# Last projection of a decoder step with the tokens stationary and the rows of b_w_out streaming

## Chip, cores and metric

The kernel runs on one core of a Trainium2 chip. The metric is the device time of the whole program in microseconds (us), as the median of several runs. The engines are PE (TensorE: PE its matmuls, PEld its weight loads), ACT (ScalarE), DVE (VectorE), POOL (GpSimd) and SP (SyncE, which here only issues DMAs). Every engine works through its own instructions in order and waits on semaphores for the others.

## What is computed

One inference step of a two-layer decoder: 512 prompt tokens and 8 sample tokens, model width 1024, float32. Layer 0 is a state-space mixer, layer 1 a dilated attention with a gate. The change touches the end of layer 1 alone:

```python
    o = o.reshape(bsz, seq_len, ATTN_WIDTH).astype(x.dtype) * jax.nn.silu(z)
    return x + rms_norm(o @ w_out, norm_post)
...
def rms_norm(x, g):
    xf = x.astype(jnp.float32)
    y = xf * lax.rsqrt(jnp.mean(xf * xf, axis=-1, keepdims=True) + RMS_EPS)
    return (y * g.astype(jnp.float32)).astype(x.dtype)
```

Here `o` is 520 tokens by 1024, `w_out` (the input b_w_out) 1024 by 1024, and the mean runs over the 1024 outputs of a token. The results y_prompt and y_sample are token rows of 1024.

## The kernel before, in words

**Number format.** Every large product is made of three: operands are split into a high part (fp32r, a copy by ACT) and a low part (the difference to the original, a subtraction by POOL for weights and by DVE for activations), and PE adds high x high, high x low and low x high in PSUM.

**Layout.** Activations lie with channels on the 128 partitions and the 520 tokens along the row. The residual stream is `xT`, 8 tiles of 128 channels x 520 tokens. PSUM holds two accumulators of 1024 columns (`acc`) and four of 512 (`aux`).

**A projection before** (class `Dense`, lines 76 to 194). Weights come in units of 128 x 1024 (8 blocks of 128 inputs x 128 outputs) into two slots `raw`; ACT makes `w_hi` (L104), POOL `w_lo` (L109), and PE multiplies with the weight block stationary and the tokens moving in two cuts of 256 and 264 columns (L161, in the mixer L1950). One unit gives one output tile of 128 channels: 8 blocks x 3 terms x 2 cuts = 48 matmuls. Units alternate between the two slots and the two accumulators.

**The mixer** (function `mixer`, L1539 on) holds the kv projection, the q projection with the attention of the prompt, the gate projection (tiles Z0 to Z0+7) and, spread among them, the attention of the 8 sample tokens. Its order is written out by hand, tile by tile and slot by slot, for each engine. At its end:
- SP issues the v rows of the sample attention (`v_rows`), and before the last four of them it waits for POOL's last splits, to load the first two units of b_w_out (L1782).
- PE runs `value_rows(0)` between the last two gate tiles and `value_rows(1)` after the last (L1900, L1903: 32 columns of probabilities stationary, 512 columns moving), then `pick_heads` (L1913: 128 x 128 stationary, 8 columns moving, 16 products that the trace shows as 32 matmuls).
- DVE makes `ot` = attention x gate (`gate`, L2050) and the low part `ylo` (`low`, L2054), ACT the high part `yhi` (`high`, L2239). The sample's columns come last: `pick_heads`, a copy (L2154), the gate (L2158), the high part (L2289), the low part (L2160).

**After the mixer** come two functions with blocks of their own, and between blocks the engines meet:
- `attn_out` calls `residual` (L1379): 8 units of b_w_out as above. DVE copies each output tile out of PSUM (L1497), ACT squares it (L284), and PE sums the squares over the channels by a product with a matrix of ones (L290), one tile behind. Then ACT takes the root (L298), DVE the reciprocal for 520 tokens (L305), and for each of the 8 tiles a scaling (L1503) and the addition to `xT` (L1509).
- `write_y` (L2297) turns `xT` back into token rows: per block of 128 tokens 8 transposes on PE (L2319), a copy by ACT or DVE (L2327, L2335; L2329 for the sample), and SP stores it in two DMAs (L2343), the sample in one (L2345). SP's last wait is for all stores and for the copy of the cache.

## Time and profile before

| what | us |
|---|---|
| median of 3 runs (1497.32 to 1501.45) | 1498.37 |
| the profiled execution: its own time | 1499.59 |
| the profiled execution: its span, first to last instruction | 1497.8 |
| PE busy in the span | 1324.4 |
| DVE / POOL / ACT busy | 669.6 / 493.5 / 484.5 |

The profile is of one execution. Times in the rows count from the start of the span. Busy time of PE is modelled, since matmuls are pipelined: the pitch between starts tells more than the length of one. PEclk (the granted clock) is TensorE's clock as a share of full speed. A timeline row is: start, length, engine, line, operation, output <- inputs, shapes, count, and in brackets the idle time before it and what ended it. Lengths of merged rows (x2, x8) run from the first start to the last end, so the pitch of repeated work is the distance of two starts.

### The profile page before, as it was taken

How to read it: one execution, taken by the hardware profiler on the slowest of the kernel's cores; microseconds unless marked ns; L12 is line 12 of the kernel's file. 1: busy time of each engine (PE TensorE's matmuls, PEld its weight loads, DVE VectorE, ACT ScalarE, POOL GpSimd, SP SyncE). 2: the span in 40 equal slices, each digit the busy share in tenths (PEclk: the TensorE clock that was granted, in tenths of full speed). 3: DMA queues.
4: the chain of work that ended last, by engine and by line, in shares of the span. 5: the costliest groups of instructions: out<-in, count | busy, mean ns of one | idle time of the engine just before them, and what ended most of it. 6: DMA issues, size and time to landing. Idle time of an engine off the chain costs nothing. (4 is left out here: it accounts for less than half of the span.)

```text
span 1497.8 us, 29253 instructions
## 1 busy us (share of the span) xinstructions
PE 1324.4 (88%) x11957; PEld 1256.3 (84%) x11957; DVE 669.6 (45%) x1121; ACT 484.5 (32%) x820; POOL 493.5 (33%) x296
## 2 busy tenths in 40 slices
PE   4988869979989999999997996799968888889893
PEld 4988869969879999999997995799857777778792
DVE  5865568949611212212110006561246666766214
ACT  4233333325522222222221223232334444444121
POOL 2222100000033434443432331233346665664230
PEclk9999989989999999999998998899979999999897
DMA  8588854421223333333332251134767778784111
GB/s 187 97 139 137 138 92 126 135 86 34 61 78 101 110 96 107 96 107 102 101 100 70 84 141 28 43 96 143 219 204 249 269 250 290 245 299 132 67 56 57
DMA packets 254406, 193.69 MB, mean 129 GB/s; under 512 B 44600, under 2 KB 240080, under 8 KB 253552
## 3 DMA queue, kind: packets, MB, share of 16 engines
q1 hardware_dynamic: 253520, 158.95, 40.1%
q10 hardware_dynamic: 800, 33.53, 6.2%
q8 instruction: 61, 1.00, 0.3%
q14 instruction: 25, 0.20, 0.0%
HBM read 172.08 MB, written 53.87 MB: 151 GB/s over the span
## 5 line engine op out<-in xcount | busy, mean ns | idle before, releaser
L109 POOL TENSOR_TENSOR w_lo<-raw,w_hi 128x1024 fp32r<-128x1024 f32 x154 | 369.0, 2398 | 839.9 <-ACT w_hi L104 556.3
L161 PE MATMUL acc<-act_hi,w_hi 128*128 128x256 f32 x1728 | 354.7, 287 | 22.5 <-POOL w_lo L109 10.2
L161 PE MATMUL acc<-act_lo,w_hi 128*128 128x256 f32 x1728 | 352.6, 286 | 0.0
L161 PE MATMUL acc<-act_hi,w_lo 128*128 128x256 f32 x1728 | 352.0, 285 | 0.0
L161 PEld LDWEIGHTS acc<-act_hi,w_hi 128*128 128x128 f32 x1728 | 272.0, 191 | 25.4 <-issue 16.8
L104 ACT ACTIVATE w_hi<-raw 128x1024 fp32r<-128x1024 f32 x156 | 164.6, 1056 | 373.7 <-PE acc L161 290.4
L161 PEld LDWEIGHTS acc<-act_hi,w_lo 128*128 128x128 f32 x1728 | 272.2, 191 | 0.0
L161 PEld LDWEIGHTS acc<-act_lo,w_hi 128*128 128x128 f32 x1728 | 272.0, 191 | 0.0
L1364 DVE SCALAR_TENSOR_TENSOR sig<-acc,vec,sig 128x520 f32<-128x520 f32 x16 | 12.1, 759 | 293.5 <-PE acc L161 293.5
L1950 PE MATMUL acc<-act_hi,w_hi 128*128 128x256 f32 (+1 forms) x512 | 113.3, 304 | 33.0 <-ACTq L2210 29.3
L1950 PEld LDWEIGHTS acc<-act_hi,w_hi 128*128 128x128 f32 x512 | 81.1, 195 | 41.3 <-ACTq L2210 34.5
L1950 PE MATMUL acc<-act_lo,w_hi 128*128 128x256 f32 (+1 forms) x512 | 105.6, 289 | 0.0
L1950 PE MATMUL acc<-act_hi,w_lo 128*128 128x256 f32 (+1 forms) x512 | 105.2, 288 | 0.0
L1795 POOL TENSOR_SCALAR scores<-scores,prob_scale 128x384 f32<-128x384 f32 x64 | 81.2, 1268 | 6.3
L1950 PEld LDWEIGHTS acc<-act_lo,w_hi 128*128 128x128 f32 x512 | 82.0, 194 | 0.0
L1950 PEld LDWEIGHTS acc<-act_hi,w_lo 128*128 128x128 f32 x512 | 81.8, 194 | 0.0
L2025 DVE SCALAR_TENSOR_TENSOR scores<-near_distances,neg_slopes,acc 128x256 f32<-128x256 f32 x64 | 30.4, 474 | 102.5 <-PE acc L1848 102.3
L1793 POOL TENSOR_TENSOR scores<-scores 128x128 f32<-128x128 f32 x64 | 39.4, 616 | 92.2 <-DVE prob_scale L2040 92.2
L2226 ACT ACTIVATE scores<-scores,neg_max 128x512 f32<-128x512 f32 x64 | 46.2, 722 | 57.3 <-DVE neg_max L2034 57.3
L161 PE MATMUL acc<-y_hi,w_hi 128*128 128x256 f32 (+1 forms) x256 | 54.0, 293 | 10.0 <-issue 6.1
L2234 ACT ACTIVATE probsT<-aux 128x384 f32<-128x384 f32 x64 | 31.4, 491 | 91.4 <-PE aux L1858 71.4
L161 PE MATMUL acc<-y_lo,w_hi 128*128 128x256 f32 (+1 forms) x256 | 52.6, 287 | 0.0
(311 smaller groups left out, 1953.3 us busy)
## 6 DMA issues: line engine op xcount, KB each, us to landing
raw<-a_w_glu SPq DMA_DIRECT2D x64, 512.0 KB, 4.0
s_kv<-cache_kv ACTq DMA_DIRECT2D x8, 4088.0 KB, 15.2
raw<-a_w_in SPq DMA_DIRECT2D x32, 512.0 KB, 4.2
raw<-b_w_in SPq DMA_DIRECT2D x32, 512.0 KB, 4.3
q_spread<-scratch_q SPq DMA_DIRECT2D x16, 768.0 KB, 7.4
raw<-a_w_out SPq DMA_DIRECT2D x16, 512.0 KB, 4.0
raw<-w_kv SPq DMA_DIRECT2D x16, 512.0 KB, 4.0
k_rows<-cache_kv SPq DMA_DIRECT2D x32, 256.0 KB, 8.3
```

Of the source, the lines that this page charges most:

```text
L104: act.activation(self.mem.wh[s][:, :, :], self.mem.raw[s][:, :, :], ACT.Copy).then_inc(self.hi_ready, 1)
L109: pool.tensor_tensor(self.mem.wl[s][:, :, :], self.mem.raw[s][:, :, :], self.mem.wh[s][:, :, :].bitcast(F32), ALU.subtract).then_inc(self. ...
L161: ins = nc.tensor.matmul(mem.acc[a][:, 256 + lo:256 + hi], w[s][:, k, :], x[:, k0 + k, lo:hi], start=first and k == 0 and i == 0, stop=las ...
L1364: v.scalar_tensor_tensor(sg[s][:, :], columns(mem.acc[1]), mem.vec[:, bass.ds(V_BGLU + i, 1)], sg[s][:, :], ALU.add, ALU.mult).then_inc(dn ...
L1793: pool.tensor_tensor(x[:, 2, :], x[:, 2, :], x[:, 3, :], ALU.add).then_inc(scaled, 1)
L1795: pool.tensor_scalar(x[:, 0:3, :], x[:, 0:3, :], linv[:, i:i + 1], None, ALU.mult).then_inc(scaled, 1)
L1950: ins = nc.tensor.matmul(acc[a][:, 256 + lo:256 + hi], w[t % 2][:, k, :], x[:, k, lo:hi], start=k == 0 and i == 0, stop=k == 7 and i == 2)
L2025: v.scalar_tensor_tensor(x[:, 0:2, :].rearrange("p a k -> p (a k)"), near[:, r, :], slope[:, head:head + 1], src[:, 0:256], ALU.mult, ALU. ...
L2226: act.activation(x, x, ACT.Exp, scale=-1.0, bias=nmin[:, i:i + 1], accum_out=lsum[:, i:i + 1]).then_inc(exped, 1)
L2234: act.activation(PT[h][:, r, :, :], aux[n % 2][:, 0:3 * P].rearrange("p (c x) -> p c x", c=3), ACT.Copy).then_inc(p_moved, 1)
```

## The change

- The last projection moves into the mixer's block; `attn_out` and `write_y` go. The 128 tokens of a block are now stationary (`yhi`, `ylo`), and rows of b_w_out move, 512 columns at a time: the result is 128 tokens x 1024 outputs in PSUM. There are five blocks of tokens (starts 0, 128, 256, 384 and 392: the last overlaps its neighbour by 120 tokens, so that the 8 sample tokens have a full block), each 8 x 3 x 2 = 48 matmuls of 512 columns.
- All 8 row blocks of b_w_out (128 x 1024 each) are kept on chip, in places that are free by then. SP loads block 0 after the last bias, 1 and 2 after POOL's last splits, 3 to 7 after the last gate tile. ACT makes the high parts; POOL makes the low parts of 0 to 3, DVE those of 4 to 7, in place.
- PE goes over the 8 rows with the first two token blocks together, right after `value_rows(1)`; `pick_heads` comes after row 0, and after rows 1 to 5 the residual of one token block is turned into token rows (`turn_x`: 8 transposes into two `aux` joined as `pair`), moved to SBUF by ACT (`move_x`). Then the other three blocks follow, all 8 rows each.
- Per block ACT squares the 1024 outputs with a running sum and takes the root of one number per token; DVE inverts it, scales by it and by the gains in token rows (`grow`, loaded by a broadcast DMA) and adds the residual, in two halves of 512; SP stores each half (two DMAs for a prompt block, one for the sample).
- SP's last four `v_rows` no longer stand behind a load of b_w_out.

```diff
--- before.py
+++ after.py
@@ -1561,6 +1561,7 @@
     for s in range(2):
         t, o = mem.at(f"probsT{s}", [P, 4, 3, P], o)
         PT.append(t)
+    near_at = o
     near, o = mem.at("near_distances", [P, 4, 2 * P], o)
     far, o = mem.at("far_distances", [P, 2, P], o)
     slope, o = mem.at("neg_slopes", [P, 3 * N_HEADS], o)
@@ -1578,6 +1579,7 @@
     scol, o = mem.at("slope_column", [P, 3], o)
     pick, o = mem.at("sequence_of_row", [P, NS], o)
     st, o = mem.at("d_stats", [P, 4], o)
+    prod_at = o
     prod, o = mem.at("d_products", [P, 3, HALF, P], o)
     qrow, _ = mem.at("q_rows", [3 * NS, P], 1408)
 
@@ -1603,6 +1605,27 @@
     joined = [mem.at("d_joined0", [P, D], a)[0], mem.at("d_joined1", [P, D], vt_at)[0]]
     assert a + half <= pt_at + 2 * 4 * 3 * P * 4
 
+    raw_at = [near_at, mem.ring_at, mem.ring_at + half, mem.ring_at + 4 * half]
+    high_at = [prod_at, mem.ring_at + 2 * half, mem.ring_at + 3 * half, mem.ring_at + 5 * half]
+    for at in (mem.acth_at, mem.actl_at):
+        for i in range(2):
+            raw_at.append(at + DT * TOK * 4 + 2 * half * i)
+            high_at.append(at + DT * TOK * 4 + 2 * half * i + half)
+    wo = [mem.at(f"w_out{k}", [P, D], raw_at[k])[0] for k in range(DT)]
+    wol = [mem.at(f"w_out_lo{k}", [P, D], raw_at[k], F32R)[0] for k in range(DT)]
+    woh = [mem.at(f"w_out_hi{k}", [P, D], high_at[k], F32R)[0] for k in range(DT)]
+    xr, a = mem.at("x_rows", [P, 5, D], mem.rest)
+    prow = []
+    for s in range(2):
+        t, a = mem.at(f"y_part{s}", [P, D], a)
+        prow.append(t)
+    grow, a = mem.at("gain_rows", [P, D], a)
+    ysq, a = mem.at("y_squares", [P, D], a)
+    ysum, a = mem.at("y_sums", [P, 8], a)
+    yroot, a = mem.at("y_roots", [P, 8], a)
+    yrstd, a = mem.at("y_rstd", [P, 8], a)
+    assert a <= r_end
+
     ot, _ = mem.at("attn_out", [P, DT, TOK], mem.acth_at)
     kR, _ = mem.at("k_residue", [P, DT, TOK], mem.acth_at)
     zb, _ = mem.at("zb", [P, DT, TOK], mem.actl_at)
@@ -1614,8 +1637,9 @@
     const = ten["constants"]
     cache = ten["cache_kv"].rearrange("s t z h d -> s t z (h d)")
     wk, wb = blocks(ten["w_kv"]), blocks(ten["b_w_in"][0, :, :])
-    w_out = blocks(ten["b_w_out"][0, :, :])
-    mem.b_out = nxt = Dense(nc, mem, "b_out", 1, [w_out[:, :, cols(n)] for n in range(2)])
+    token = [0, P, 2 * P, 3 * P, TOK - P]
+    order = [0, 1, 2, 4, 3]
+    home = [acc[0], acc[1], mem.pair[1], acc[0], acc[1]]
 
     def weights(t):
         if t < 2 * DT:
@@ -1675,6 +1699,11 @@
         dv_full, dv_moved, do_full = sem("d_values"), sem("d_values_moved"), sem("d_out_full")
         ys_ready, ys_hi, ys_lo = sem("y_sample"), sem("y_sample_hi"), sem("y_sample_lo")
         dve = sem("dve_chain")
+        wo_in = [sem(f"w_out_in{k}") for k in range(DT)]
+        wo_hi, wo_lo, wo_lo_v = sem("w_out_hi"), sem("w_out_lo_pool"), sem("w_out_lo_dve")
+        xr_full, xr_moved, g_in = sem("x_rows_full"), sem("x_rows_moved"), sem("gain_rows_in")
+        r_full, r_squared, r_rooted, r_read = sem("y_rows_full"), sem("y_squared"), sem("y_rooted"), sem("y_rows_read")
+        r_scaled, r_ready, r_stored = sem("y_scaled"), sem("y_ready"), sem("y_stored")
         block = ctx.enter_context(nc.Block())
 
         @block.sync
@@ -1777,12 +1806,38 @@
             sp.dma_start(vnew[:, :], ten["s_kv"][:, SEQ - 1, 1, :, :].rearrange("s h d -> s (h d)")).then_inc(vn_in, 16)
             for n in range(9, 12):
                 v_rows(n)
-            for n in range(2):
-                sp.wait_ge(dn.lo_ready, TILES + n + 1)
-                sp.dma_start(mem.raw[n][:, :, :], nxt.first[n]).then_inc(nxt.landed[n], 16)
+            def load_out(k):
+                sp.dma_start(wo[k][:, :], ten["b_w_out"][0, P * k:P * k + P, :]).then_inc(wo_in[k], 16)
+
+            def store_rows(n):
+                i, at = order.index(n), token[n]
+                yp = ten["y_prompt"][0, :, :].rearrange("(c j) d -> j c d", j=L)
+                for h in range(2):
+                    sp.wait_ge(r_ready, 2 * i + h + 1)
+                    half = slice(512 * h, 512 * h + 512)
+                    if n < 4:
+                        for j in range(2):
+                            sp.dma_start(yp[2 * n + j, :, half], xr[64 * j:64 * j + 64, n, half]).then_inc(r_stored, 16)
+                    else:
+                        sp.dma_start(ten["y_sample"][:, 0, half], xr[P - NS:P, n, half]).then_inc(r_stored, 16)
+
+            sp.wait_ge(biased, UNITS)
+            load_out(0)
             sp.wait_ge(scored, 6 * DT)
             for n in range(12, 2 * NS):
                 v_rows(n)
+            for k in range(1, 3):
+                sp.wait_ge(dn.lo_ready, TILES + k)
+                load_out(k)
+            sp.wait_ge(dn.unit_read, TILES + 2)
+            for k in range(3, DT):
+                load_out(k)
+            sp.wait_ge(dv_full, 4)
+            sp.dma_start(grow[:, :], ten["b_norm_post"][0:1, :].broadcast_to([P, D])).then_inc(g_in, 16)
+            for n in order:
+                store_rows(n)
+            sp.wait_ge(r_stored, 16 * 18)
+            sp.wait_ge(mem.cache_moved, 16 * NS)
 
         @block.gpsimd
         def _(pool):
@@ -1803,7 +1858,9 @@
                             finish_unit(n)
                 if t + 2 < TILES:
                     dn.split_lo(pool, t + 2, t % 2)
-            nxt.split_lo_first(pool)
+            for k in range(4):
+                pool.wait_ge(wo_hi, k + 1)
+                pool.tensor_tensor(wol[k][:, :], wo[k][:, :], woh[k][:, :].bitcast(F32), ALU.subtract).then_inc(wo_lo, 1)
 
         @block.tensor
         def _(pe):
@@ -1983,8 +2040,50 @@
                 if t == Z0 + 6:
                     value_rows(0)
             value_rows(1)
-            pick_heads(0)
-            pick_heads(1)
+
+            def out_products(k, i):
+                at = token[order[i]]
+                for w, x, first, last in ((woh, mem.yhi, True, False), (wol, mem.yhi, False, False),
+                                          (woh, mem.ylo, False, True)):
+                    for c in range(0, D, 512):
+                        ins = nc.tensor.matmul(home[i][:, c:c + 512], x[:, k, at:at + P], w[k][:, c:c + 512],
+                                               start=first and k == 0, stop=last and k == DT - 1)
+                if k == DT - 1:
+                    ins.then_inc(r_full, 1)
+
+            def turn_x(n):
+                if n == 1:
+                    pe.wait_ge(ys_ready, 1)
+                elif n >= 2:
+                    pe.wait_ge(xr_moved, n - 1)
+                for f in range(DT):
+                    ins = nc.tensor.transpose(mem.pair[n % 2][:, cols(f)], mem.xT[:, f, token[n]:token[n] + P],
+                                              mem.ident[:, :])
+                ins.then_inc(xr_full, 1)
+
+            pe.wait_ge(z_ready, DT)
+            for k in range(DT):
+                pe.wait_ge(y_lo, k + 1)
+                if k < 4:
+                    pe.wait_ge(wo_lo, k + 1)
+                else:
+                    pe.wait_ge(wo_lo_v, k - 3)
+                for i in range(2):
+                    out_products(k, i)
+                if k == 0:
+                    pick_heads(0)
+                    pick_heads(1)
+                if 1 <= k < 6:
+                    turn_x(k - 1)
+            for i in range(2, 5):
+                if i == 2:
+                    pe.wait_ge(xr_moved, 4)
+                else:
+                    pe.wait_ge(r_read, i - 2)
+                if order[i] == 4:
+                    pe.wait_ge(ys_lo, 1)
+                for k in range(DT):
+                    out_products(k, i)
 
         @block.vector
         def _(v):
@@ -2159,8 +2258,23 @@
             v.wait_ge(ys_hi, 1)
             v.tensor_tensor(mem.ylo[:, :, SEQ:TOK], y_s[:, :, :], mem.yhi[:, :, SEQ:TOK].bitcast(F32),
                             ALU.subtract).then_inc(ys_lo, 1)
-            v.wait_ge(ys_lo, 1)
-            v.wait_ge(y_lo, DT)
+            for k in range(4, DT):
+                v.wait_ge(wo_hi, k + 1)
+                v.tensor_tensor(wol[k][:, :], wo[k][:, :], woh[k][:, :].bitcast(F32), ALU.subtract).then_inc(wo_lo_v, 1)
+            v.wait_ge(g_in, 16)
+            for i, n in enumerate(order):
+                v.wait_ge(r_rooted, i + 1)
+                link(v.reciprocal(yrstd[:, i:i + 1], yroot[:, i:i + 1]))
+                v.wait_ge(xr_moved, n + 1)
+                for h in range(2):
+                    half = slice(512 * h, 512 * h + 512)
+                    ins = v.scalar_tensor_tensor(prow[i % 2][:, half], home[i][:, half], yrstd[:, i:i + 1],
+                                                 grow[:, half], ALU.mult, ALU.mult)
+                    ins.then_inc(r_scaled, 1)
+                    v.wait_ge(r_scaled, 2 * i + h + 1)
+                    if h:
+                        v.sem_inc(r_read, 1)
+                    v.tensor_tensor(xr[:, n, half], xr[:, n, half], prow[i % 2][:, half], ALU.add).then_inc(r_ready, 1)
 
         @block.scalar
         def _(act):
@@ -2237,6 +2351,16 @@
             def high(f):
                 act.wait_ge(gated, f + 1)
                 act.activation(mem.yhi[:, f, 0:SEQ], ot[:, f, 0:SEQ], ACT.Copy).then_inc(y_hi, 1)
+
+            def out_high(k):
+                act.wait_ge(wo_in[k], 16)
+                if k < 3:
+                    act.wait_ge(scored if k == 0 else dn.unit_read, 6 * DT if k == 0 else TILES + 1)
+                act.activation(woh[k][:, :], wo[k][:, :], ACT.Copy).then_inc(wo_hi, 1)
+
+            def move_x(n):
+                act.wait_ge(xr_full, n + 1)
+                act.activation(xr[:, n, :], mem.pair[n % 2][:, :], ACT.Copy).then_inc(xr_moved, 1)
 
             nm.apply_hi(act, 0)
             for t in range(2 * DT):
@@ -2276,75 +2400,26 @@
                         act.activation(zb[:, f, :], zb[:, f, :], ACT.Silu).then_inc(z_ready, 1)
                 for f in {Z0 + 5: (0, 1, 2), Z0 + 6: (3, 4), Z0 + 7: (5, 6)}.get(t, ()):
                     high(f)
+                if t == Z0 + 6:
+                    for k in range(3):
+                        out_high(k)
                 if t == Z0 + 7:
                     move_values(0)
-            for n in range(2):
-                act.wait_ge(nxt.landed[n], 16)
-                act.wait_ge(dn.unit_read, TILES + n + 1)
-                act.activation(mem.wh[n][:, :, :], mem.raw[n][:, :, :], ACT.Copy).then_inc(nxt.hi_ready, 1)
-                if n == 0:
-                    high(DT - 1)
+            high(DT - 1)
             move_values(1)
+            out_high(3)
             act.wait_ge(ys_ready, 1)
             act.activation(mem.yhi[:, :, SEQ:TOK], y_s[:, :, :], ACT.Copy).then_inc(ys_hi, 1)
-
-
-def attn_out(nc, mem, ten, dram):
-    residual(nc, mem, "b_out", mem.b_out, ten["b_w_out"][0, :, :], 1, mem.yhi[:, :, :], mem.ylo[:, :, :], V_BPOST,
-             mem.rest, mem.rest + DT * TOK * 4)
-
-
-def write_y(nc, mem, ten, dram):
...
+            for k in range(4, DT):
+                out_high(k)
+                move_x(k - 4)
+            move_x(4)
+            for i in range(5):
+                act.wait_ge(r_full, i + 1)
+                act.activation(ysq[:, :], home[i][:, :], ACT.Square, accum_out=ysum[:, i:i + 1]).then_inc(r_squared, 1)
+                act.wait_ge(r_squared, i + 1)
+                act.activation(yroot[:, i:i + 1], ysum[:, i:i + 1], ACT.Sqrt, scale=1.0 / D,
+                               bias=mem.cst[:, 0:1]).then_inc(r_rooted, 1)
 
 
 INS = ["x_prompt", "x_sample", "state_s5_re", "state_s5_im", "cache_kv", "a_norm_pre", "a_w_in", "a_lam_re",
@@ -2366,10 +2441,10 @@
     }
     with ExitStack() as ctx:
         mem.acc = [ctx.enter_context(nc.psum_tensor(f"acc{a}", [P, 1024], F32)) for a in range(2)]
-        mem.aux = [ctx.enter_context(nc.psum_tensor(f"aux{a}", [P, 512], F32)) for a in range(4)]
+        mem.pair = [ctx.enter_context(nc.psum_tensor(f"aux{a}", [P, 1024], F32)) for a in range(2)]
+        mem.aux = [mem.pair[a // 2][:, 512 * (a % 2):512 * (a % 2) + 512] for a in range(4)]
         mem.cache_moved = nc.alloc_semaphore("cache_moved")
-        parts = (intake, gate_and_scan, outputs, glu, ssm_out,
-                 mixer, attn_out, write_y)[:phases]
+        parts = (intake, gate_and_scan, outputs, glu, ssm_out, mixer)[:phases]
         for group in (parts[:2], parts[2:]):
             with nc.cleanup_on_exit():
                 for f in group:
```

## Rows read from the trace of the kernel before

**Rows 1.** The page, part 1: busy time, share of the span, instructions.
```profile
PE 1324.4 (88%) x11957; PEld 1256.3 (84%) x11957; DVE 669.6 (45%) x1121; ACT 484.5 (32%) x820; POOL 493.5 (33%) x296
```

**Rows 2.** Stretches of the end: busy time and count of each engine, granted clock, DMA.
```profile
core 0: us, PE busy (x) PEld busy (x) DVE busy (x) ACT busy (x) POOL busy (x), PEclk, DMA share, GB/s
...
1393.75:1399.50 5.75, 5.75 (x49) 1.14 (x48) 3.67 (x4) 4.65 (x7) 2.25 (x1) 1.00 0.00 0
1399.50:1402.00 2.50, 1.11 (x14) 1.11 (x10) 1.28 (x2) 0.60 (x1) 2.50 (x2) 0.97 0.00 0
1402.00:1409.60 7.60, 5.04 (x24) 4.95 (x24) 0.90 (x4) 0.26 (x1) 0.38 (x1) 0.50 0.00 0
1409.60:1415.20 5.60, 5.53 (x25) 5.56 (x26) 0.00 (x0) 0.00 (x0) 0.00 (x0) 0.50 0.67 187
1415.20:1463.70 48.50, 48.50 (x385) 47.80 (x384) 4.90 (x7) 10.41 (x13) 14.40 (x6) 1.00 0.15 44
1463.70:1482.80 19.10, 2.19 (x10) 1.25 (x8) 15.15 (x18) 2.76 (x4) 0.00 (x0) 0.67 0.00 0
1482.80:1488.00 5.20, 5.06 (x25) 4.86 (x26) 1.23 (x1) 1.20 (x2) 0.00 (x0) 0.58 0.19 41
```

**Rows 3.** Timeline from the last value rows to the first product of the projection.
```profile
1396.62 1.92 PE L1900 MATMUL aux<-v_rows,d_probsT 128*32 128x512 f32 x16
...
1398.47 1.06 PE L1903 MATMUL aux<-v_new,p_new 8*32 8x512 f32 x8
...
1400.92 6.12 PE L1913 MATMUL aux<-ident,d_joined 128*128 128x8 f32 x32 [1.39 <-DVE d_joined L2102]
...
1407.83 0.26 ACT L2289 ACTIVATE o_hi<-gated_sample 128x64 fp32r<-128x64 f32 x1 [7.63 <-DVE gated_sample L2158]
...
1409.67 0.78 PE L161 MATMUL acc<-o_hi,w_hi 128*128 128x256 f32 x2 [2.63 <-PEq L116]
```

**Rows 4.** Timeline, PE: neighbouring pairs of products, at either clock.
```profile
1411.11 0.64 PE L161 MATMUL acc<-o_hi,w_hi 128*128 128x256 f32 x2
1411.55 0.64 PE L161 MATMUL acc<-o_lo,w_hi 128*128 128x256 f32 x2
...
1426.21 0.40 PE L161 MATMUL acc<-o_hi,w_hi 128*128 128x256 f32 x2
1426.45 0.40 PE L161 MATMUL acc<-o_lo,w_hi 128*128 128x256 f32 x2
```

**Rows 5.** Timeline of the norm: the reciprocal, the first scaling and addition of 8.
```profile
1467.59 3.40 DVE L305 RECIPROCAL b_out_post_rstd<-b_out_post_root 128x520 f32<-128x520 f32 x1 [2.86 <-ACT b_out_post_root L298]
1471.03 0.76 DVE L1503 SCALAR_TENSOR_TENSOR b_out_post_tmp<-b_out_o,vec,b_out_post_rstd 128x520 f32<-128x520 f32 x1
1471.83 0.70 DVE L1509 TENSOR_TENSOR xT<-xT,b_out_post_tmp 128x520 f32<-128x520 f32 x1
```

**Rows 6.** Timeline of the end: eight transposes at full clock, and the stores.
```profile
1485.91 6.98 SPq L2343 DMA_DIRECT2D y_prompt<-y_rows  x8
...
1487.84 0.85 PEld L2319 LDWEIGHTS acc<-ident,xT 128*128 128x128 f32 x8 [0.29 <-DVE y_rows L2335]
...
1492.93 0.68 SPq L2345 DMA_DIRECT2D y_sample<-y_sample_rows  x1
```

**Rows 7.** Timeline of the kernel's start: squares with a sum, and a root.
```profile
18.61 1.06 ACT L559 ACTIVATE x_squares<-xtok 128x1024 f32<-128x1024 f32 x1 [0.35 <-DMA xtok<-x_prompt]
19.57 0.19 ACT L559 ACTIVATION_READ_ACCUMULATOR x_squares<-xtok 128x1 f32 x1
19.79 0.30 ACT L561 ACTIVATE x_roots<-x_sums,cst 128x5 f32<-128x5 f32 x1
```

**Rows 8.** Timeline: a split on POOL and a subtraction on DVE beside it.
```profile
1378.18 2.40 POOL L109 TENSOR_TENSOR w_lo<-raw,w_hi 128x1024 fp32r<-128x1024 f32 x1 [3.91 <-ACT w_hi L104]
...
1378.66 2.47 DVE L2054 TENSOR_TENSOR o_lo<-attn_out,o_hi 128x512 fp32r<-128x512 f32 x1 [1.18 <-ACT o_hi L2239]
```

**Rows 9.** DMA issues from 1360 us on: count, KB each, us to landing.
```profile
raw<-b_w_out SPq DMA_DIRECT2D x8, 512.0 KB, 4.0
```

More of the change, by code:

```diff
@@ L2287, in _ @@
             move_values(1)
+            out_high(3)
             act.wait_ge(ys_ready, 1)
             act.activation(mem.yhi[:, :, SEQ:TOK], y_s[:, :, :], ACT.Copy).then_inc(ys_hi, 1)
-def attn_out(nc, mem, ten, dram):
-    residual(nc, mem, "b_out", mem.b_out, ten["b_w_out"][0, :, :], 1, mem.yhi[:, :, :], mem.ylo[:, :, :], V_BPOST,
-             mem.rest, mem.rest + DT * TOK * 4)
-def write_y(nc, mem, ten, dram):
-    yo, o = mem.at("y_rows", [P, 4, D], mem.acth_at)
-    ys, o = mem.at("y_sample_rows", [NS, D], o)
-    acc = mem.acc
-    with ExitStack() as ctx:
-        def sem(x):
-            return nc.alloc_semaphore(f"write_{x}")
-        full, moved_a, moved_v, stored = sem("transposed"), sem("moved_act"), sem("moved_dve"), sem("stored")
-        block = ctx.enter_context(nc.Block())
-        @block.tensor
-        def _(pe):
-            for n in range(5):
-                if n >= 2:
-                    pe.wait_ge(moved_a if n % 2 == 0 else moved_v, n // 2)
-                for f in range(DT):
-                    if n < 4:
-                        out, src = acc[n % 2][:, P * f:P * f + P], mem.xT[:, f, P * n:P * n + P]
-                    else:
-                        out, src = acc[0][0:NS, P * f:P * f + P], mem.xT[:, f, SEQ:TOK]
-                    ins = nc.tensor.transpose(out, src, mem.ident[:, :])
-                ins.then_inc(full, 1)
-        @block.scalar
-        def _(act):
-            for n in (0, 2, 4):
-                act.wait_ge(full, n + 1)
-                if n < 4:
-                    act.activation(yo[:, n, :], acc[0][:, :], ACT.Copy).then_inc(moved_a, 1)
-                else:
-                    act.activation(ys[:, :], acc[0][0:NS, :], ACT.Copy).then_inc(moved_a, 1)
-        @block.vector
-        def _(v):
-            for n in (1, 3):
-                v.wait_ge(full, n + 1)
-                v.tensor_copy(yo[:, n, :], acc[1][:, :]).then_inc(moved_v, 1)
-        @block.sync
-        def _(sp):
-            yp = ten["y_prompt"][0, :, :].rearrange("(c j) d -> j c d", j=L)
-            for n in range(4):
-                sp.wait_ge(moved_a if n % 2 == 0 else moved_v, n // 2 + 1)
-                for i in range(2):
-                    sp.dma_start(yp[2 * n + i], yo[64 * i:64 * i + 64, n, :]).then_inc(stored, 16)
-            sp.wait_ge(moved_a, 3)
-            sp.dma_start(ten["y_sample"][:, 0, :], ys[:, :]).then_inc(stored, 16)
-            sp.wait_ge(stored, 16 * 9)
-            sp.wait_ge(mem.cache_moved, 16 * NS)
```

## Prediction

> **What bounds the kernel now.** I read the page first: PE is busy for 88% of the span [rows 1], so in the middle of the kernel only less work on PE would help, and the change leaves that alone. Then I cut the end into stretches [rows 2], because an average says nothing of a stage. The reader is to see three things there. From 1415.2 to 1463.7 us PE is busy all the time: this stage is bound by products. From 1463.7 to 1482.8 PE does 2.2 us of work in 19.1 and DVE 15.2: here a chain of small steps on DVE decides. From 1482.8 to the end at 1497.8 come transposes, copies and stores. So of the 98.3 us between the last value rows (1398.47 + 1.06 = 1399.53 us [rows 3]) and the end, the last 34.1 follow the last product. Between 1399.5 and 1409.67 there is a second chain: `pick_heads` until 1407.04, the sample's gate and split, the change of block, and only then the first product [rows 3], at half clock for the first 5.6 us [rows 2].
>
> **What goes.** Everything after 1399.53: 10.1 us of chain in front, 54.0 us of projection, 34.1 us of norm, transposes and stores. The new end is laid out from the same instant; what stands before it on PE is unchanged. I price it term by term.
>
> **Products, 52.6 us.** There are 5 x 8 x 3 x 2 = 240 of 512 columns, 122,880 columns in place of 384 products with 99,840. At half clock a pair with 520 columns takes 1411.55 - 1411.11 = 0.44 us (0.433 over longer stretches), 0.83 ns per column; at full clock 1426.45 - 1426.21 = 0.24 us, 0.46 ns per column instead of half of 0.83 [rows 4]. So at full clock each product costs some 12 ns beyond its streaming. If that is a thing per product that wider ones hide (at half clock nothing of it is seen), 512 columns take 512 x 0.4165 = 213 ns; if it is a fixed addition, 225; if it grows with the columns, 237. The row at half clock, where one product lasts about as long (217 ns) as a wide one at full clock, speaks for the low end, so I take the middle of the first two, 219 ns: 240 x 0.219 = 52.6 us, bounds 51.2 and 57.0.
> The Trainium skill (TensorE: Matmul & The Clock Gate, Back-to-back issue gap) puts sustained streams of 512 columns at about 131 ns each; by that the products would take 31.4 us. The trace speaks against it, with 120 ns for 260 columns.
>
> **`pick_heads`, 4.0 us.** Its 32 matmuls cost 0.11 us each in the stretch at 0.97 of the clock and 0.21 us at half clock [rows 2]. They now follow 2.6 us of products without the gap of 1.4 us before them. Bounds 2.6 (the best half microsecond of that stretch; at 0.11 it is 3.5) and 6.1 us (as now); I take 4.0, with the clock falling on the way.
>
> **Turning the residual, 5.3 us.** Five times 8 transposes: their loads take 0.85 us at full clock [rows 6], 1.05 with the start of the next stage. Bounds 4.3 and 6.4.
>
> **Joints, 0.8 us.** Some 14 places where PE passes from one kind of work to another, at a few hundredths each; bounds 0.3 and 2.0, the upper one from 0.14 us a place.
>
> **Clock, 2.0 us.** After `pick_heads` the clock was at 0.50 for 5.6 us of dense products before it rose [rows 2], which is 2.8 us lost. Whether it falls at all now is open, since PE doesn't stop: bounds 0 and 2.8.
>
> **Does PE have to wait for weights?** Rows 0 to 2 are split before the last gate tile ends. Rows 3 to 7 are issued when it ends, at 1393.8 us; a load of 512 KB lands in 4.0 us [rows 9], so five of them are there by about 1406, with nothing else on the queue. Each row then needs ACT (1.06 us for 1024 columns, by the square in [rows 7]), DVE (two times 0.70, by [rows 5]) and a residual move on ACT (about 1.1): 2.1 us on ACT per row against 5.3 + 1.05 us that PE takes per row. Row 4 is ready at about 1412, PE wants it at 1417. So this costs nothing; its cover is 5 us of lead and 4 us per row. The row that POOL splits (row 3) is ready by 1404. POOL's three early splits can hold up DVE, as a subtraction on DVE took 2.47 us and ended behind one of 2.40 on POOL [rows 8]: the gates and low parts of tiles 4 to 6 may lose up to 5 us at 1386 to 1393, where DVE otherwise idles and nothing of PE asks for them; I cost it at nothing.
>
> **New waits and the queues.** SP: the last four `v_rows` go out some 13 us earlier, so `value_rows(1)` can only gain, and it didn't wait before. What stands behind SP's new waits are only later weights, gains and stores. ACT: behind its wait for the sample's gate stand rows 4 to 7, and the gate comes about 1 us after `pick_heads`, at 1408 us, some 9 us before PE wants row 4. PE: the fourth block waits until DVE has read the first; that is read about 6 us after it is complete (square, table load, root, reciprocal, two scalings), while the third block gives 10.5 us of cover. The gain rows are 512 KB (4.0 us [rows 9]) and wanted 25 us after they are issued.
>
> **The tail after the last product, 11.1 us.** Square and running sum 1.25 us, root 0.30 [rows 7] (table loaded with the first block), reciprocal of one column and joints 0.55 in place of 3.40, then two halves of scaling and addition, 2 x 1.4 us [rows 5]: 4.9. Then SP: eight stores took 6.98 us to issue, 0.87 each [rows 6]; the last two need 2.0 us with what is left of the two before them. From the end of the last issue (1492.93 + 0.68 = 1493.61 us) to the end of the span, 4.2 us now [rows 6], taken over unchanged. Sum 11.1; bounds 10 and 12.5. The other four blocks' norms and stores (4 issues of 0.87 us per 10.5 us of products) lie beside products.
>
> **Sum.** 52.6 + 4.0 + 5.3 + 0.8 + 2.0 = 64.7 us, so the last product ends at 1399.5 + 64.7 = 1464.2, about where it ends now: the earlier start pays for more columns and the transposes. With the tail the span ends at 1475.3, 22.5 us before 1497.8. The gain is the tail: 34 us become 11. The profiled execution's own time is 1499.59, 1.8 us around its span and 1.2 above the median; against the median of 1498.4 the forecast is 1498.4 - 22.5 = 1475.9, so 1476 us. All lower bounds give 1399.5 + 58.4 + 10 = 1468 in the span, all upper ones 1399.5 + 74.3 + 12.5 = 1486.
>
> **Rivals.**
> *Wide products are slow (slower).* The only 512-column work in the trace are the value rows: 16 records in 1.85 us (1396.62 to 1398.47 [rows 3]), and as they load 32 columns each and four can stand side by side, one pass could cost up to 0.46 us. If 512 moving columns of fp32r cost that, the products take 240 x 0.46 = 110 us and the time is 1476 + 58 = 1534. It decides from 52.6 + 22.5 = 75 us, 313 ns per product. For it: same width. Against it: those are plain float32, the projection's are fp32r, and those run at 0.46 ns per column at 256 and 264 [rows 4]; the price per column would have to double. 5%.
> *The clock stays at half through the first two blocks (no change).* `pick_heads` and five rounds of transposes lie among the first 96 products. If these keep the clock at 0.50 from about 1404 us on, 84 products at 0.43 in place of 0.22 us and the transposes lose 22 us, 2 of them in the sum already: 1476 + 20 = 1496. Against it: from 1482.8 on only transposes ran, and the clock rose nevertheless (0.58 over 5.2 us from a start at 0.50 [rows 2]). 4%. The Trainium skill (TensorE: Matmul & The Clock Gate, PE-mode transpose) says that transposes don't count as busy for this gate; the rise among transposes here differs from it.
> *Weights come late.* The chain over ACT and DVE for rows 4 to 7, or the five loads, take twice what I think; then PE stands some 4 us in the first part: 1480. For it: ACT, DVE and PE hand rows and residual blocks to each other in turn. Against it: the cover above. 8%.
> *Neighbouring wide products overlap (faster still).* If a product costs 120 ns by itself, whatever its width up to 512, the products take 240 x 0.12 = 28.9 us: 1476 - 24 = 1452. For it: the 12 ns beyond streaming are unexplained. Against it: no row shows more columns per time than [rows 4] do, and at half clock the pitch goes with the columns. 3%. The 131 ns of the Trainium skill's page above would give 1455.
> *The tail doesn't shrink as said.* Stores hold the end: 18 issues of 0.87 us are 16 us in all, but 14 of them lie under products. This is in the upper bound of the tail.
>
> **Numbers.** My forecast as summed has 80%: 1476, with 1468 to 1486 of its own. Late weights (8%) lie inside that range; the other three, 12% together, lie outside, and I widen the top by 1 us only: 1468 to 1487. Differences under 0.3%, 4.5 us, are about what a measurement can't tell from no change. Faster: 80 + 8 + 3 = 91%; same: 4%; slower: 5%.
>
> **What would show each step.** In the new profile: a pitch of 213 to 225 ns between neighbouring products at full clock; a first product at about 1399.6 us; granted clock near 1.00 from 1410 on; no wait of PE for a low part from row 1 on, nor for a block being read; the last product near 1464; DVE's last addition some 5 us later; the end some 11 us after the last product. I am wrong if the pitch is over 300 ns, if PE waits for rows for more than 5 us in all, or if the stores of earlier blocks are still queued on SP when the last block is ready.

## The result, and the profile of the changed kernel

The changed kernel takes 1475.02 us (median of 4 runs, 1471.09 to 1475.38), the kernel before, measured beside it, 1499.91 (1497.32 to 1502.99): a ratio of 0.9827, 95% interval 0.98 to 0.9854. In a later set, with more runs, it took 1479.16 (5 runs, 1476.27 to 1483.96) against 1499.69 (9 runs): 0.9853, 0.9825 to 0.9881. Forecast were 1476, range 1468 to 1487.

Part 1 of the page answers to [rows 1]: there are 176 fewer instructions on PE, and it is busy for 9 us less.

```profile
PE 1315.2 (90%) x11781; PEld 1239.0 (84%) x11781; DVE 669.8 (46%) x1123; ACT 488.1 (33%) x827; POOL 484.2 (33%) x292
```

The chain of waits of the changed kernel, from the last value rows on (start us, us, what). It is laid out from the same instant as the forecast: the value rows end at 1393.17 + 0.99 = 1394.16 us.

```profile
1393.17 0.99 PE aux L1960 x8
1394.16 2.99 PE acc L2049 x12
1397.15 3.47 PE aux L1970 x32
1400.62 4.45 PE acc L2049 x12
1405.07 0.88 PE aux L2060 x8
1405.94 2.80 PE acc L2049 x12
...
1419.75 0.87 PE aux L2060 x8
1420.62 5.55 PE acc L2049 x24
1426.17 11.15 PE aux L2049 x48
1437.32 22.33 PE acc L2049 x96
...
1459.67 1.12 ACT y_squares L2419 x2
...
1463.64 0.69 DVE x_rows L2277
```

The reader is to see that every line from 1394.16 to 1459.65 is PE's, and that each begins where the one before ends. The 10.1 us between value rows and first product [rows 3] are gone: the first product starts at once, `pick_heads` (32 matmuls on line 1970) stands after the first row's 12 products, and the turning of the residual (line 2060) between the rows. Behind the last product stands one block's norm, 4.7 us, where the DVE chain of [rows 2] and [rows 5] was. The windows of the same stretch answer to [rows 2] (columns as there):

```profile
core 0: us, PE busy (x) PEld busy (x) DVE busy (x) ACT busy (x) POOL busy (x), PEclk, DMA share, GB/s
1388.40:1394.16 5.76, 5.76 (x50) 1.21 (x49) 3.19 (x5) 2.87 (x5) 0.45 (x1) 1.00 0.71 215
1394.16:1400.47 6.31, 6.31 (x44) 5.78 (x45) 0.00 (x0) 1.55 (x2) 2.38 (x1) 1.00 0.75 303
1400.47:1404.70 4.23, 4.23 (x14) 3.36 (x14) 2.12 (x5) 1.20 (x2) 0.00 (x0) 0.60 0.00 0
1404.70:1420.40 15.70, 15.70 (x91) 13.27 (x89) 3.68 (x3) 6.94 (x7) 0.00 (x0) 1.00 0.00 1
1420.40:1459.60 39.20, 39.20 (x171) 31.41 (x168) 11.76 (x20) 7.84 (x14) 0.00 (x0) 1.00 0.18 42
1459.60:1464.33 4.73, 0.04 (x1) 0.00 (x0) 2.96 (x5) 1.41 (x3) 0.00 (x0) 0.75 0.08 18
1464.33:1469.00 4.67, 0.00 (x0) 0.00 (x0) 0.01 (x1) 0.00 (x0) 0.00 (x0) 0.50 0.41 94
```

PE is busy for the whole of each stretch up to 1459.6. The granted clock is 1.00 but for 4.2 us behind `pick_heads`, at 0.60. Of the end, 4.7 us belong to DVE and ACT and the last 4.7 to the stores. SP's timeline of the end, which answers to [rows 6]:

```profile
1462.86 1.11 SPq L1820 DMA_DIRECT2D y_prompt<-x_rows  x2
1464.36 1.10 SPq L1820 DMA_DIRECT2D y_prompt<-x_rows  x2
```

**Where the time went.** From the end of the value rows to the last product it is 1459.65 - 1394.16 = 65.5 us, from there to the end of the span 9.4; before, the two were 64.2 and 34.1. So the section that the change touches went from 98.3 to 74.8 us, 23.4 less. The profiled executions differ by 1499.59 - 1471.09 = 28.5 us. The other 5 come from ahead of the change: the value rows end at 1394.16 and not 1399.53. That is no effect of the change. SP issues the load of `v_new` ahead of everything that the change touches, and it stands 5.37 us earlier too, as much as the end of the value rows (the kernel before, then the changed one):

```profile
1366.16 0.30 SPq L1777 DMA_DIRECT2D v_new<-s_kv  x1
...
1360.79 0.30 SPq L1806 DMA_DIRECT2D v_new<-s_kv  x1
```

In another profile of the same changed kernel the value rows end at 1402.20, and over all profiles of this study with the change, whose work up to there is the same, at 1394 to 1406. From here on sections are compared, counted from the end of the value rows, since whole times carry these differences along.

### The profile page after: what moved, and what is told of

Read it like the earlier page. It is cut to its first block and busy times, and to the rows that moved or that the text cites. A ratio compares the mean times of both kernels' runs of the same rounds, so it can differ in the third digit from the quotient of the medians.

```text
span 1469.0 us, 28793 instructions
## 1 busy us (share of the span) xinstructions
PE 1315.2 (90%) x11781; PEld 1239.0 (84%) x11781; DVE 669.8 (46%) x1123; ACT 488.1 (33%) x827; POOL 484.2 (33%) x292
## 5 line engine op out<-in xcount | busy, mean ns | idle before, releaser
L109 POOL TENSOR_TENSOR w_lo<-raw,w_hi 128x1024 fp32r<-128x1024 f32 x146 | 349.8, 2397 | 783.8 <-ACT w_hi L104 519.8
L104 ACT ACTIVATE w_hi<-raw 128x1024 fp32r<-128x1024 f32 x150 | 158.5, 1057 | 342.2 <-PE acc L161 256.4
L1364 DVE SCALAR_TENSOR_TENSOR sig<-acc,vec,sig 128x520 f32<-128x520 f32 x16 | 12.1, 759 | 295.1 <-PE acc L161 295.1
L2340 ACT ACTIVATE scores<-scores,neg_max 128x512 f32<-128x512 f32 x64 | 46.3, 723 | 55.8 <-DVE neg_max L2133 55.8
```

Source lines behind the costliest of these rows:

```text
L104: act.activation(self.mem.wh[s][:, :, :], self.mem.raw[s][:, :, :], ACT.Copy).then_inc(self.hi_ready, 1)
L109: pool.tensor_tensor(self.mem.wl[s][:, :, :], self.mem.raw[s][:, :, :], self.mem.wh[s][:, :, :].bitcast(F32), ALU.subtract).then_inc(self. ...
L2340: act.activation(x, x, ACT.Exp, scale=-1.0, bias=nmin[:, i:i + 1], accum_out=lsum[:, i:i + 1]).then_inc(exped, 1)
```

## The experiments

The theory before the runs: the projection runs without a gap at 232.5 ns per product, 9% above half of what 512 columns cost at half clock (512 x 0.833 / 2 = 213 ns [rows 4]); the clock falls behind `pick_heads`, whose matmuls have 8 columns, and would not if products broke it up; and the tail is one block's norm and its stores. The rivals stand in the expectations.

**1. `pick_heads` ahead of the first row.**

```diff
             pe.wait_ge(z_ready, DT)
+            pick_heads(0)
+            pick_heads(1)
             for k in range(DT):
...
-                if k == 0:
-                    pick_heads(0)
-                    pick_heads(1)
```

> pick_heads stands before the first row of weights, as in the order before the change; nothing else differs. All times are counted from the end of the last value rows; in the changed kernel the last product ends 65.5 us after it. Theory (the place of pick_heads hides a chain and spares the clock): a gap of 0.7 to 1.4 us for the copies, pick_heads partly at half clock (up to 6.1 us instead of 3.5) and then up to 5.6 us of dense products at half clock instead of about 3: the last product ends 4 to 6 us later, at 69.5 to 71.5. Rival (only the gap counts, the clock takes care of itself): 1 to 1.4 us later, at 66.5 to 66.9.

The section to the last product took 67.99 us (1403.38 to 1471.37), the tail 9.33. Windows of this run, columns as above:

```profile
1403.38:1404.19 0.81, 0.00 (x1) 0.03 (x1) 0.00 (x0) 0.74 (x2) 0.00 (x0) 1.00 1.02 384
1404.19:1409.30 5.11, 5.11 (x33) 5.11 (x34) 0.00 (x0) 0.80 (x1) 2.34 (x1) 0.70 0.61 246
1409.30:1416.76 7.46, 7.46 (x27) 5.90 (x27) 2.12 (x5) 1.21 (x2) 0.00 (x0) 0.75 0.00 0
```

A gap of 0.81 us in which PE waits for `pick_heads`' input, `pick_heads` at 0.70 of the clock in 5.11, and the next 24 products at 0.75 in 7.46: 13.4 us for what takes 2.99 + 3.47 + 4.45 = 10.9 in the changed kernel. The gain of putting a row of products ahead is 2.5 us, between the two forecasts. So neither forecast came true as it stands. Of the 2.5 us the gap is 0.8 and the slower `pick_heads` 1.6; the 24 products behind it took 7.46 us, as rows 0 and 1 do in the changed kernel (2.99 + 4.45), so there the clock cost nothing more, where the theory had put more than 1 us.

**2. `pick_heads` split: 16 matmuls behind row 0, 16 behind row 1.**

```diff
-                if k == 0:
-                    pick_heads(0)
-                    pick_heads(1)
+                if k < 2:
+                    pick_heads(k)
```

> pick_heads in two halves, one after row 0 and one after row 1. Theory (the clock falls because 3.5 us of matmuls with 8 moving columns stand together): halves of 1.7 us between products of 2.8 us leave the granted clock at 1.00 throughout, and the last product ends 1.5 us earlier, 64.0 us after the value rows. Rival (the fall belongs to the instant, not to the run of small matmuls, or the sample's later chain costs a wait): the clock still falls for about 3 us and the last product ends at 65.5 us or later.

63.89 us to the last product, tail 9.3. One window over the whole of it:

```profile
1403.90:1467.79 63.89, 63.87 (x312) 52.63 (x312) 17.56 (x28) 17.41 (x25) 2.38 (x1) 1.00 0.17 49
```

The same 312 instructions on PE, the clock at 1.00 throughout, and 1.6 us less than in the changed kernel (65.5): that is what the fall of the clock cost there, row 1 in 4.45 us where later rows take 2.80. In two more profiles with the split (experiments 9 and 11) it didn't fall either.

**3. Products of 256 columns, 480 of them.**

```diff
-                    for c in range(0, D, 512):
+                    for c in range(0, D, 256):
...
```

> The same products in moving pieces of 256 columns in place of 512: 480 matmuls. Measured before: 120.5 ns at a mean of 260 columns and about 233 ns at 512. Theory A (a small fixed part of some 5 ns and 0.445 ns per column): pitch 119 ns, all products 57.0 us in place of 55.8, the last product 1 us later. Theory B (all by the column): 116 ns, no difference. Theory C (a fixed addition of 20 ns per matmul to streaming at 0.417 ns per column): 126 ns, the last product 4 to 5 us later.

The line of the chain with the last 192 products, of this run:

```profile
1446.02 22.72 PE acc L2049 x192
```

118.3 ns each, against 22.33 / 96 = 232.6 at 512 columns. A line through the two is 4 ns per product and 0.4465 ns per column. So almost nothing goes with the product; the price goes with the columns and is 7% above half of the 0.833 ns that a column costs at half clock [rows 4]. The whole took 66.51 us, 1.0 more than with 512 columns. What the prediction called "a fixed addition" and "a thing per product that wider ones hide" are both out. The pairs of [rows 4] fit the line: 2 x 4 + 520 x 0.4465 = 240 ns.

**4. Only the products of the two high parts; the two with a low part are left out.**

```diff
-                for w, x, first, last in ((woh, mem.yhi, True, False), (wol, mem.yhi, False, False),
-                                          (woh, mem.ylo, False, True)):
+                for w, x, first, last in ((woh, mem.yhi, True, True),):
```

> The two products with a low part are left out (their splits and waits stay): 80 products in place of 240. Theory (PE bounds this stage and rows of weights are ready long before they are wanted): 160 x 0.233 = 37.2 us come off, less 1 to 2 us of waiting for the first block to be read before its PSUM is used again; the last product ends 28 to 30 us after the value rows. Rival (ACT and DVE, which split four rows and move five blocks of the residual in turn, set the pace of rows 1 to 7 with 2.1 us or more per row and a chain between them): the first part takes 5 us or more longer than its products and transposes, the last product ends at 34 us or later.

The time was 1442.24 us and the section 31.4 us (1398.67 to 1430.1), a little over the theory's 28 to 30. Windows of this run, over the first rows and the rest:

```profile
1398.67:1417.05 18.38, 18.38 (x104) 16.54 (x104) 5.79 (x8) 10.38 (x12) 2.34 (x1) 0.81 0.22 89
1417.05:1430.10 13.05, 11.91 (x50) 8.96 (x49) 9.50 (x17) 6.81 (x13) 0.00 (x0) 1.00 0.43 100
```

All the waits of PE in its section (engine, tile, line and what was waited for: us in total, times, longest):

```profile
PE acc L2048 <- DVEq L2275: 1.1, 1, 1.1
```

With a third of the products, a row of weights is wanted every 1.8 us, and PE still never waits for one. Its one wait, 1.1 us, is for DVE to read the first block, the very wait that the prediction named as covered. The rest of the excess is the clock, 0.81 in the first part: `pick_heads` 5.00 us in place of 3.47, row 1 1.91 for its four products in place of 0.93 (4 x 232.5 ns), the first turn 1.70 in place of 0.87, 3.3 us together. So late weights are no rival with all the products in place, and the time goes with the products.

**5. The sample's projection left out, with its block's norm.**

```diff
-    order = [0, 1, 2, 4, 3]
-    home = [acc[0], acc[1], mem.pair[1], acc[0], acc[1]]
+    order = [0, 1, 2, 3]
+    home = [acc[0], acc[1], mem.pair[1], acc[0]]
...
-            for i in range(2, 5):
+            for i in range(2, 4):
```

> The block of the 8 sample tokens is left out of the projection (its rows are stored without the projection's part); the other four blocks are as they were. Theory (PE is the bound up to the last product, and 8 tokens cost as much as 128, since the moving columns set the price): 48 products of 0.2325 us come off, the last product ends 54.3 us after the value rows in place of 65.5, and the tail stays at 9.4 us. Rival (the fourth prompt block then waits for the first to be read, or stores pile up): the gain is under 9 us.

55.98 us to the last product, 9.5 less than in the changed kernel; 11.2 of it is the block, exactly 48 products. The chain of this run shows what ate the difference:

```profile
1401.57 3.82 PE aux L1972 x32
1405.39 5.32 PE acc L2051 x12
1410.71 1.25 PE aux L2062 x8
...
1443.37 11.19 PE acc L2051 x48
```

`pick_heads`, row 1 and the first turn took 3.82 + 5.32 + 1.25 us and not 3.47 + 4.45 + 0.88: the clock was low for longer, which cost 1.6 us, and so the theory's 54.3 was missed. The block with the eight new tokens thus costs 11.2 us, as much as one with 128, because the weights are what moves: all 1024 columns of each row pass for any block. It does have 128 stationary tokens, 120 of them computed twice; that fewer would not make it cheaper is shown down to 64, by experiment 8.

**6. Norm and stores in whole rows of 1024.**

```diff
-                for h in range(2):
-                    half = slice(512 * h, 512 * h + 512)
+                for h in range(1):
+                    half = slice(0, D)
...
```

> Norm, addition and store of a block in one piece of 1024 columns, not two halves of 512. Theory (the halves buy next to nothing: DVE's work is the same 2.9 us in two instructions instead of four, and SP's last two issues follow the last addition either way): the span ends within 0.5 us of the 9.4 us after the last product. Rival (the halves let two stores go out 1.4 us sooner, and the end hangs on the bytes stored last): the tail is 1 to 2 us longer.

The tail was 9.76 us against 9.35, within the theory's 0.5. From the chain of this run:

```profile
1402.07 3.47 PE aux L1970 x32
1405.54 2.89 PE acc L2049 x12
...
1464.74 1.30 DVE y_part L2271
...
1466.18 1.22 DVE x_rows L2276
```

And from SP's timeline, its last issues:

```profile
1467.43 1.11 SPq L1820 DMA_DIRECT2D y_prompt<-x_rows  x2
```

The 0.4 us are the difference of two effects. The norm is shorter in one piece: one scaling of 1.30 us and one addition of 1.22 end 4.4 us after the last product, two of each at 0.7 end 4.7 us after it. The last two issues take the same, 1.11 us here and 1.10 there, but each now stores 256 KB instead of 128, and from their end to the end of the span it is 4.3 us in place of 3.5. So the end does hang a little on what is stored last, as the rival had it, but for 0.7 us and not 1 to 2. The first two lines hold a surprise: row 1 took 2.89 us, so the clock did not fall here, though nothing about `pick_heads` was changed.

**7. The sample's block last.**

```diff
-    order = [0, 1, 2, 4, 3]
+    order = [0, 1, 2, 3, 4]
```

> The sample's block is computed and stored last, the fourth prompt block before it; the last stores are then two of 16 KB in place of four of 128 KB. Theory (the tail after the last addition is issue and landing of the last stores): two issues less, 1.3 us, of which the second half's lie on the path: the tail is 0.6 to 1.3 us shorter, 8.1 to 8.8 us. Rival (the tail is fixed from the last addition on): 9.4 us.

The tail took 7.91 us, a little below the forecast, and the part before it 65.52, unchanged. The last block's store is now one issue per half, of 16 KB, where two of 128 KB went out; experiment 9 shows it again.

**8. Only 64 of each block's tokens stationary; the other half of the projection is left out.**

```diff
-                        ins = nc.tensor.matmul(home[i][:, c:c + 512], x[:, k, at:at + P], w[k][:, c:c + 512],
+                        ins = nc.tensor.matmul(home[i][0:64, c:c + 512], x[:, k, at:at + 64], w[k][:, c:c + 512],
```

> Only 64 of each block's 128 tokens are stationary (the other half of the projection is left out); the moving side is as it was. Theory A (the 20 ns by which a 512-wide product exceeds 512 x 0.4165 ns go with the moving columns): pitch stays at 232 to 233 ns and the last product stays at 65.5 us. Theory B (they come from loading the stationary side): half the load, 223 ns or less, the last product at 63.2 us or earlier.

The last 96 products in the chain of this run:

```profile
1448.83 22.20 PE acc L2049 x96
```

231.3 ns each, 232.6 with 128 tokens, while the load of the stationary operand went from 0.188 to 0.134 us (medians of PEld's instructions). Theory B had 223 or less, so loading is not what makes up the surplus, the 19 ns between 213 and 232.5.

**9. Split and sample last together, 10. the changed kernel and 11. the split alone again, all on one chip.** The edit of 9 is that of 2 with that of 7.

> Both small changes together: pick_heads in two halves after rows 0 and 1, and the sample's block last. Theory (a run of 3.5 us of matmuls with 8 columns is what lets the clock fall, and the last stores' number and size set the tail): granted clock 1.00 from the value rows to the last product, which ends 63.9 us after them, then 7.9 us to the end of the span: 71.8 us in place of 74.9 in the changed kernel, so about 3 us less in the median. Rival (where the clock falls is a matter of the instant, not of the run): the clock falls here for 3 us too and only the 1.5 us of the tail come off.

> The changed kernel as it is, once more, beside the version with both small changes. Theory: from the value rows to the last product 64 to 67 us, depending on whether and for how long the clock falls after pick_heads, 9.4 us after it; the time about 3 us above the version with both. What stands before the value rows varies by some us from run to run in either, without a cause in the change. Rival: the stretch is the same 65.5 us to a few tenths in every execution.

> pick_heads in two halves once more, the rest as in the changed kernel. Theory (the run of small matmuls decides): clock 1.00 throughout again, the last product 63.9 us after the value rows. Rival (chance): the clock falls after one of the halves and the last product ends at 65 us or later.

Windows of 9, up to the last product, to the last addition and to the end:

```profile
1400.52:1464.43 63.91, 63.89 (x312) 52.63 (x312) 17.55 (x28) 17.41 (x25) 2.38 (x1) 1.00 0.21 60
1464.43:1469.10 4.67, 0.00 (x0) 0.00 (x0) 2.95 (x5) 1.41 (x3) 0.00 (x0) 0.92 0.02 4
1469.10:1472.40 3.30, 0.00 (x0) 0.00 (x0) 0.01 (x1) 0.00 (x0) 0.00 (x0) 0.50 0.03 5
```

Windows of 10, `pick_heads` and then row 1:

```profile
1405.19:1408.97 3.78, 3.78 (x33) 3.78 (x33) 0.00 (x0) 0.00 (x0) 1.08 (x1) 0.90 0.30 122
1408.97:1413.13 4.16, 4.16 (x15) 3.26 (x15) 2.12 (x5) 1.20 (x2) 0.00 (x0) 0.68 0.00 0
```

The window of 11 up to the last product:

```profile
1400.02:1463.91 63.89, 63.87 (x312) 52.66 (x312) 17.56 (x28) 17.41 (x25) 2.38 (x1) 1.00 0.17 50
```

Both gains add up: 63.9 + 8.0 = 71.9 us in 9, against 65.5 + 9.3 = 74.8 in 10. Behind the last addition there are 3.3 us in 9 and 4.7 in the changed kernel; of the difference 0.8 is the one issue of 0.31 us (SP, from 1469.13 on) in place of two in 1.10. As a whole 9 takes 1474.52 us (5 runs, 1470.51 to 1476.4), a ratio to before of 0.9818 (0.9793 to 0.9843); 10 takes 1479.16 in the same set. The medians are 4.6 us apart; the sections account for 2.9, and 1.7 are that the value rows end at 1400.52 in the one profile and 1402.20 in the other. The intervals of the two ratios overlap, so the verdict on the two rests on the sections: the version with both edits is faster than the kernel before by its ratio, and by about 3 us than the changed one in the profiled sections.

## Why the prediction came out right

The forecast was 75.8 us from the end of the value rows to the end, 22.5 less than before; measured were 74.8 and 23.4. Term by term, us:

| term | forecast | bounds | measured |
|---|---|---|---|
| 240 products | 52.6 | 51.2 to 57.0 | 55.8 |
| `pick_heads` | 4.0 | 2.6 to 6.1 | 3.5 |
| turning the residual | 5.3 | 4.3 to 6.4 | 4.4 |
| joints | 0.8 | 0.3 to 2.0 | 0.2 |
| clock | 2.0 | 0 to 2.8 | 1.65 |
| to the last product | 64.7 | | 65.5 |
| tail | 11.1 | 10 to 12.5 | 9.4 |

**The products** are the term that was mis-sized, by 3.2 us: 240 x 232.5 ns. The step that failed is "so I take the middle of the first two, 219 ns". Of the three readings of [rows 4] the third, growth with the columns (237), was the near one, and experiment 3 shows it: 4 ns and 0.4465 per column. The reason that I gave for the low end, that a product at half clock takes 217 ns and shows no addition, was a comparison by duration; the surplus isn't tied to duration but to the columns at full clock. The changed kernel has products of 512 columns at half clock too, right behind `pick_heads`:

```profile
1401.42 1.06 PE L2049 MATMUL acc<-w_out_lo,o_hi 128*128 128x512 f32 x2
...
1402.28 1.06 PE L2049 MATMUL acc<-w_out_hi,o_lo 128*128 128x512 f32 x2
```

A pair takes 1402.28 - 1401.42 = 0.86 us, 0.43 per product and 0.84 ns per column, the price of the narrow ones at half clock, with nothing on top. At full clock the same product takes 232.5 ns, 19 more than the 213 that half of this price gives (512 x 0.833 / 2). The upper bound of 57.0 held the term. By the list of what would show each step the pitch was to be 213 to 225 ns, and it was 232.5.

**`pick_heads`, turns, joints and clock** came to 12.1 forecast and 9.7 measured. 3.47 us for `pick_heads` is the 0.11 per matmul of the stretch at 0.97 [rows 2], because the clock lasted until it was nearly done; the fall came behind it and cost row 1 4.45 - 2.80 = 1.65 us, where I had 2.0 and "open whether it falls at all". With `pick_heads` split the fall stayed away in three profiles of three (experiments 2, 9 and 11), with it in one piece behind row 0 in one of eight (experiment 6): the split very likely takes it away, but the spared one shows that more than the order of the work decides. Turns take 0.87 each, the loads' 0.85 [rows 6] and nearly nothing more. Joints are what is left, 65.5 - 55.8 - 3.5 - 4.4 - 1.65 = 0.2: hardly any cost for PE to pass from one kind of work to another, and less than the lower bound of 0.3.

**Waits.** PE had no wait in the section, for weights or for a block; experiment 4 showed the margin. My path to that was only partly right. Counted from the end of the value rows, the five loads had landed after 6.3 us at the latest (no DMA traffic from 1400.47 on), where I had 6.5, though a load took longer than the 4.0 I had put, 7.4 us in the median, with several under way at once. POOL's split of row 3 ended after 4.1 us (1398.23), where I had 4.5. Row 4's low part was done on DVE after 9.7 us (1403.88), where I had 12.5, and PE wanted it after 19.1. One sum of the prediction is wrong: it sets 5.3 + 1.05 us of PE against 2.1 of ACT per row, but a row is 12 products here and not 24, so PE takes 2.80 + 0.87 = 3.67 us and the cover is 1.6 us per row and not 4. What kept PE from waiting was the lead, 9.4 us at row 4. POOL's three early splits did hold up DVE, as said [rows 8]: two of its operations took 2.9 us in place of 0.7, some 4.4 us in all, and nothing of PE asked for them. POOL's early splits in the timeline of the changed kernel:

```profile
1380.47 8.38 POOL L1863 TENSOR_TENSOR w_out_lo<-w_out,w_out_hi 128x1024 fp32r<-128x1024 f32 x3 [5.25 <-ACT w_out_hi L2359]
```

And DVE's, with the two operations beside them and row 4's low part:

```profile
1380.93 2.87 DVE L2153 TENSOR_TENSOR o_lo<-attn_out,o_hi 128x512 fp32r<-128x512 f32 x1
1383.73 2.88 DVE L2149 TENSOR_TENSOR attn_out<-attn_out,zb 128x512 f32<-128x512 f32 x1
...
1402.65 1.23 DVE L2263 TENSOR_TENSOR w_out_lo<-w_out,w_out_hi 128x1024 fp32r<-128x1024 f32 x1 [0.72 <-ACT w_out_hi L2359]
```

**The tail** was forecast 1.7 us too high, and what it measured lies under its lower bound of 10. The norm came as said, 4.7 for 4.9. What stood on SP was overpriced: behind the last addition (1464.33) two issues take 1.1 us, 0.55 each and not 0.87, and none was left over from the half before, whose pair ended at 1463.97; I had 2.0. From the end of the last issue to the end of the span it was 3.5 us and not 4.2 [rows 6].

**The rivals.** Wide products at 0.46 us each: out, 232 ns. The clock at half through the first two blocks: out, it was at 0.60 over 4.2 us and at 1.00 from 1404.7 to 1420.4, among transposes. Late weights: out, with experiment 4. Overlapping products: out, as the pitch is 232 ns and goes with the width in experiment 3 (the prediction's 240 x 0.12 is 28.8, not 28.9, which changes nothing).

That the time, 1475.02, lies 1 us from the forecast is partly luck: errors of +3.2 and -4.1 us cancelled, and the same kernel had a median 4 us higher in the second set.

## What to carry to other kernels

When a projection is the last thing that a kernel does, put the tokens stationary and let the weights move, so that a block of tokens is finished in rows and its norm and stores lie under the next block's products; what remains is one block's tail, 9.4 us here where the tail of everything was 34. Finish with the block that has the smallest store (some 1.4 us here), and break up stretches of narrow matmuls with dense products (1.6 us in the profiles where the clock fell). Price products by their columns at the clock that they will have, from two widths where the trace holds them; a block with few tokens costs as much as a full one in this layout (tested down to 64 stationary tokens).

## What the runs showed of the hardware that I had not expected

At the full granted clock a column of fp32r costs 0.4465 ns, 7% more than half of the 0.833 at half clock, whatever the width (256 or 512) and the number of stationary columns (64 or 128); with the 4 ns per product, 512 columns cost 9% more than half. The Trainium skill (TensorE: Matmul & The Clock Gate, Back-to-back issue gap) gives N / 2.4 + 2.5 ns for a lone product, 216 ns for 512 columns; the trace has 232.5 in a stream. What the surplus is stays open.

`pick_heads` is 32 matmuls of 8 columns in a row, with products ahead of it and behind it and no gap in PE, and still the clock fell. A window of the changed kernel, right behind it (columns as above):

```profile
1400.62:1402.00 1.38, 1.38 (x4) 1.10 (x5) 0.90 (x4) 0.59 (x2) 0.00 (x0) 0.50 0.00 0
```

The granted clock is 0.50 there, 1.2 GHz, after PE had been busy without a break. It fell on the way or right behind in seven profiles that have `pick_heads` in one piece after row 0, and in experiment 1 with it in front; it did not in the three where products split it in two, nor in experiment 6, where it is in one piece (row 1 took 2.89 us). Why that one was spared stays open; no run was made for it.

Transposes among products kept the clock: five rounds of eight, 0.87 us each, lie in a stretch at 1.00 (1404.7 to 1420.4). The Trainium skill (same page, PE-mode transpose) says that they don't count as busy in the same way; with 4.4 us of them in those 15.7, the trace doesn't show that they hurt.

Not tried: a layout in which the eight new tokens of the sample need no pass of their own (11.2 us in experiment 5).
